# A decoder step on one core: sample scores, rank products and gate units reordered on TensorE, folded rows added on VectorE

## The reference

```python
z = h @ w_in                                   # q, k, v, conv inputs, gates
attn = sliding-window attention with sinks     # prompt blocks of 128; samples against cached keys
conv = c_b * short_conv(c_c * c_h)
h = layer_norm(ALPHA * h + (sigmoid(g_a) * (attn @ w_attn_out) + sigmoid(g_c) * (conv @ w_conv_out)) @ w_o)
eidx, gw = route(h, w_router, router_bias)     # 6 of 64 experts for each token
ffn = swiglu_shared(h) + sum over the 6 experts of gw * swiglu_e(h)
ple = sigmoid(h @ w_ple_gate) * (p @ w_ple_proj)
h = layer_norm(ALPHA * h + ffn + ple)          # the output y; keys, values and conv rows are outputs too
```

## Time and profile before

| | us |
|---|---|
| median of 3 runs | 1264.93 (1264.57 to 1266.1) |
| profiled execution, its time | 1267.28 |
| its span | 1265.4 |
| PE busy | 1227.0 (97%) |
| DVE busy | 497.9 (39%) |
| ACT busy | 306.3 (24%) |
| POOL busy | 159.8 (13%) |
| mean granted PE clock | 0.995 |

### The profile page before, as it was taken

How to read it: one execution, slowest core, us unless ns; L and a number is a source line. 1 busy time by engine, 2 the same in 40 slices (tenths; PEclk the granted TensorE clock), 3 DMA queues, 4 the chain that set the end, 5 groups by cost and what they waited for, 6 DMA issues and landing times.

```text
span 1265.4 us, 23325 instructions
## 1 busy us (share of the span) xinstructions
PE 1227.0 (97%) x8776; PEld 974.0 (77%) x8777; DVE 497.9 (39%) x1103; ACT 306.3 (24%) x560; POOL 159.8 (13%) x228
## 2 busy tenths in 40 slices
PE   7999999999999999999899999999999999999977
PEld 7988879999999999998899666556555566666643
DVE  4456574423453433566886112112112221111137
ACT  4344453322221222316012111111111111111121
POOL 0200000000000000004336121111111121211100
PEclk9999999999999999999999999999999999999999
DMA  9312122322223232606337999999999999999986
GB/s 279 103 37 67 34 68 51 80 71 79 89 68 100 67 109 76 211 21 208 141 115 305 420 419 419 421 421 419 420 421 419 420 421 418 420 421 421 421 351 264
DMA packets 98656, 307.31 MB, mean 243 GB/s; under 512 B 11244, under 2 KB 62404, under 8 KB 72840
## 3 DMA queue, kind: packets, MB, share of 16 engines
q1 hardware_dynamic: 85332, 275.20, 56.2%
q0 software_dynamic: 12304, 28.60, 5.8%
q10 hardware_dynamic: 948, 2.50, 0.6%
HBM read 294.45 MB, written 26.94 MB: 254 GB/s over the span
## 4 chain that ended last, share of the span: by engine, by line
PE 55%; DMA 37%; DVE 5%; issue 1%; DVEq 1%; ACT 0%; SPq 0%; POOL 0%; ACTq 0%; POOLq 0%
DMA w_exp<-in_w_e_down_dram 35%; PE proj L1051 32%; PE proj L1243 4%; PE proj L1384 3%; PE att L1454 2%; PE proj L1473 2%; PE att L1165 2%; PE att L1127 1%; DMA fold<-expert_rows 1%; PE att L1252 1%; PE proj L1338 1%; PE att L1178 1%; PE proj L1368 1%; PE proj L1077 1%; DVE res L2124 1%
## 5 line engine op out<-in xcount | busy, mean ns | idle before, releaser
L1454 PE MATMUL att<-w_exp,xt 128*64 128x256 f32 x2560 | 286.3, 380 | 2.7 <-DMA w_exp<-in_w_e_up_dram 2.1
L1454 PEld LDWEIGHTS att<-w_exp,xt 128*64 128x64 f32 x2560 | 207.6, 137 | 90.2 <-issue 27.5
L1051 PE MATMUL proj<-h_hi,w_hi 128*128 128x288 f32 x768 | 171.1, 304 | 0.0
L1051 PE MATMUL proj<-h_hi,w_lo 128*128 128x288 f32 x768 | 164.2, 295 | 0.0
L1051 PE MATMUL proj<-h_lo,w_hi 128*128 128x288 f32 x768 | 164.0, 295 | 0.0
L1473 PE MATMUL proj<-w_exp,ht_e 128*64 128x512 f32 x640 | 146.1, 597 | 9.6 <-DMA w_exp<-in_w_e_down_dram 4.9
L1051 PEld LDWEIGHTS proj<-h_hi,w_hi 128*128 128x128 f32 x768 | 122.0, 188 | 16.2 <-issue 15.2
L1051 PEld LDWEIGHTS proj<-h_lo,w_hi 128*128 128x128 f32 x768 | 123.5, 188 | 0.0
L1051 PEld LDWEIGHTS proj<-h_hi,w_lo 128*128 128x128 f32 x768 | 123.4, 188 | 0.0
L468 DVE TENSOR_TENSOR w_lo<-w_raw,w_hi 128x2048 fp32r<-128x2048 f32 x33 | 75.6, 2291 | 91.9 <-ACT w_hi L458 86.8
L1473 PEld LDWEIGHTS proj<-w_exp,ht_e 128*64 128x64 f32 x640 | 50.4, 136 | 77.7 <-issue 76.0
(11 more groups left out here) (384 smaller groups left out, 1810.8 us busy)
## 6 DMA issues: line engine op xcount, KB each, us to landing
w_exp<-in_w_e_gate_dram SPq DMA_DIRECT2D x64, 1024.0 KB, 16.9
w_exp<-in_w_e_up_dram SPq DMA_DIRECT2D x64, 1024.0 KB, 17.0
w_exp<-in_w_e_down_dram SPq DMA_DIRECT2D x64, 1024.0 KB, 17.1
w_raw<-in_w_in_dram SPq DMA_DIRECT2D x21, 1024.0 KB
part<-expert_rows SPq DMA_DIRECT2D x8, 1536.0 KB, 21.2
w_raw<-in_w_in_dram SPq DMA_DIRECT2D x8, 512.0 KB
w_raw<-in_w_attn_out_dram SPq DMA_DIRECT2D x8, 512.0 KB
w_raw<-in_w_conv_out_dram SPq DMA_DIRECT2D x4, 1024.0 KB
```

The source lines that it names most:

```text
L1051: last = nc.tensor.matmul(proj[:, 2 * i + a, 0:HALF], lhs, x[:, c, a * HALF:(a + 1) * HALF], start=(c == 0 and n == 0), stop=(c == KC - 1 ...
L1454: last = nc.tensor.matmul(att[e * SLOT:(e + 1) * SLOT, m, 0:FF], xt[:, c, e * SLOT:(e + 1) * SLOT], weights[e][:, c, :], start=(c == 0), s ...
```

## The change

Four edits. In the attention, PE's wait for the reading of the previous sample's scores moves from ahead of the sample scores to ahead of the prompt scores of the same step; ahead of the sample scores it waits for the one before that. In the routing, a third piece of the fourth quarter goes ahead of the rank products, and four gate units go ahead of the first table instead of three. In the end stage, DVE adds the three folded rows of tile 4 to one before it adds the sum of tile 0, and PE multiplies only that one; and a fourth row of tile 0 goes from DVE to PE.

```diff
-N_AHEAD = 3
+N_AHEAD = 4
...
-N_ON_PE = (3, 3, 4, 4)
+N_ON_PE = (4, 3, 4, 4)
...
                     if b == 0:
                         pe.wait_ge(qs_ready, 1)
-                    else:
-                        pe.wait_ge(sl_read, b)
+                    if b >= 2:
+                        pe.wait_ge(sl_read, b - 1)
                     pe.wait_ge(lg_read, n)
...
                     if n:
                         pe.wait_ge(lg_read, n)
+                    if n > 24:
+                        pe.wait_ge(sl_read, n - 24)
...
-            shared_half(1, 1, range(2))
+            shared_half(1, 1, range(3))
...
-            shared_half(1, 1, range(2, KC)).then_inc(su_ready, 1)
+            shared_half(1, 1, range(3, KC)).then_inc(su_ready, 1)
...
                 if t == NT - 1:
-                    pe.wait_ge(part_in[t], 16)
+                    pe.wait_ge(y_lo_ready, 2)
                     for half in range(2):
-                        for j in range(TOPK // 2):
-                            nc.tensor.matmul(out[:, half, :], fold_id[:, :], fold[:, j, half * 512:(half + 1) * 512],
-                                             start=(j == 0), stop=False)
+                        nc.tensor.matmul(out[:, half, :], fold_id[:, :], fold[:, 0, half * 512:(half + 1) * 512],
+                                         start=True, stop=False)
...
+            def fold_rows():
+
+                dve.wait_ge(part_in[NT - 1], 16)
+                nc.vector.tensor_tensor(fold[:, 0, :], fold[:, 0, :], fold[:, 1, :], ALU.add)
+                dve.drain()
+                nc.vector.tensor_tensor(fold[:, 0, :], fold[:, 0, :], fold[:, 2, :], ALU.add).then_inc(y_lo_ready, 1)
...
                 if s:
                     last_norm(s - 1, LAST_ORDER[s - 1])
+                if s == 0:
+                    fold_rows()
                 add_sum(s, t)
```

## The result

The changed kernel takes 1268.44 us (median of 20 runs, 1265.89 to 1270.38), the kernel before 1265.76 (20 runs, 1264.28 to 1267.25): a ratio of 1.0024, 95% interval 1.0018 to 1.0030. It is slower by a quarter of a per cent, where 1261.7 was forecast. Its runs also lie further apart, 4.5 us against 3.0. The profiled execution took 1269.49 us, span 1267.7.

What follows compares the result with a forecast made beforehand. PE bounds half of the end, transfers over a third; from 700 to 1204 the DMA engines are full. Gains of 0.77 + 0.8 (`routed`) + 1.2 + 0.5 = 3.3 us against 1264.93 gave 1261.7 us, range 1259.8 to 1264.0.

Steps and rivals of the forecast that it cites:

- the price at table 4: Routing: POOL's block 2 lies across DVE's table 4, so PE waits 1.4 us there (0 to 3.2).
- Rival (d): Routing: POOL holds table 4 for 5.2 us, PE idles 3.2, clock falls, `routed` 4.0 later: 1266.4 us; chance 0.05.
- the reorder: Routing: the moved piece and fourth unit bring PE's last table product, which releases `routed`, 2.18 us earlier before table 4's wait.
- rival (a): Routing: no collision on table 4, `routed` 2.18 us earlier: 1260.1 us; chance 0.18.
- The first table: Routing: PE's idle time ahead of the first table shrinks from 3.4 to 1.4 us; the clock stays up, gaining 2.98.
- rival (c): Routing: the clock falls in the new idle time at the first table too, 2.98 us given back: 1263.3 us; chance 0.07.
- The stream hole: Weight stream before 700: PE reaches the thin places earlier, so most of the hole closes, 1.2 us (0 to 1.4).
- Sample scores: Attention: the moved wait lets sample scores start earlier at even steps, 0.28 + 0.49 = 0.77 us (0 to 1.3).
- End stage: DVE's chain to tile 4's sum is later than PE's or even; gain 0.5 us (0.6 down to -0.4).
- rival (e): End stage: the clock stays up in most runs, so the end loses 1.1 us: 1263.3 us; chance 0.10.

Runs made afterwards that it cites:

- e1: The kernel before with the routing edits alone (third piece ahead of the ranks, four units ahead of the tables): 1.0014 of before.
- e3: The changed kernel with POOL's low part of block 2 made after unit 7 instead of unit 5: 1.0004 of before.
- e5: The changed kernel without POOL's low parts of blocks 2 and 3, ACT's copy in their place (low parts wrong): 0.9982 of before.
- e2: The changed kernel with the routing edits undone, so sample scores and end stage alone: 0.9997 of before.
- e7: The kernel before with the sample scores' edit alone: 0.9991 of before.
- e8: The kernel before with the two edits of the end stage alone: 0.9998 of before.
- e10: The kernel before with the third piece ahead of the rank products alone: 1.0003 of before.
- e6: The kernel before without POOL's low parts of blocks 2 and 3, ACT's copy in their place (low parts wrong): 0.9989 of before.
- e11: The changed kernel with POOL's low part of block 2 after unit 7 and that of block 3 behind `routed`: 1.0010 of before.
- e12: As e11, with the ranks ahead of the third piece again, as in the kernel before: 1.0003 of before.
- e16: The kernel before with the sample scores' edit and the routing edits, the end stage as before: 1.0007 of before.
- e4: As e3, with ACT's high part and POOL's low part of block 3 after unit 10 instead of unit 11: 1.0011 of before.
- e14: The changed kernel with a POOL memset of some 0.4 us ahead of block 2's low part: 1.0023 of before.
- e15: The changed kernel with a POOL memset of some 0.95 us ahead of block 2's low part: 1.0024 of before.
- e17: The kernel of e15 once more, unchanged, for a second profile: 1265.69 us in one run.
- e18: The changed kernel again, unchanged, for a third profile: 1268.2 us in one run.
- e9: The kernel before with the fourth gate unit ahead of the tables alone, the ranks as before: 1.0008 of before.

## Why the prediction was wrong, step by step

**The step that failed is the price at table 4.** The forecast was "PE waits 0.8 to 2.1 us; the bounds are 0 and POOL's whole 5.2 (3.2 of waiting). I take 1.4", with the clock untouched. The place and the mechanism were right: POOL's L708 lies across table 4, from 642.24, 28.4 us behind the ranks' copy (the forecast's 643.4 is 27.8 behind). The wait was 2.60, 2.60 and 1.99 in three profiles, inside the bounds and above the 1.4, and behind it the clock fell in two, which cost 3.06 and 1.79 more; the sum had nothing for that. POOL caught the weights ahead of the table as well, five DVE operations in all. Rival (d), which the prediction gave 0.05, is what happened in kind, though from less: it set the wait at 3.2 and its sign at an idle time of some 2.3 us, while the clock fell behind 1.99 in one execution and stayed up behind 2.60 in another. Its price, 1.5 us slower, was too low mainly for want of the second collision, below.

The trace of before could have told more: there the block had caught five operations, L1931 of the weights at 1.24 for 0.23 and the four of table 6, an excess of 3.9 us (650.57 to 656.66, less 2.23). The prediction read 2.85 from the table alone, allowed 1.3 more for the weights and took a value in the middle. With the slack of 2.0, which it had right, 3.9 is a wait of 1.9 us; the 4.5 of the changed kernel is the 2.60 measured. By the Trainium skill (SBUF — State Buffer, Who interferes with whom) a VectorE instruction with two SBUF inputs and a GpSimd one that reads SBUF shut each other out for their whole length, and a `tensor_scalar` can take the shared ports too; the trace agrees on both (1.45 for 0.44, L1932 1.35 for 0.23).

**A term was missing.** POOL's block 3 moved as well, onto DVE's last steps to `routed`: +1.5 us in the change, in e1 and in e3. I had dated block 2 against the tables and not block 3 against what lies behind them. e5 measures both collisions and the clock together: A 53.72 instead of 60.92, and 2.60 + 3.06 + 1.54 is the 7.20 between them. Against before e5's A is 2.43 shorter. The ranks come 0.8 later by the edit, so the reorder as such brings `routed` 1.6 us earlier where 2.18 was forecast, the place of rival (a).

**The first table** was right: idle 1.66 (forecast 1.4), and no low clock behind it in any profile with both routing edits, so rival (c) fell. The idle time is longer than forecast because POOL's work on the fourth unit lies on the table's last operation: L2001 took 0.99 for 0.44. The Trainium skill (TensorE: Matmul & The Clock Gate, A second HAM failure mode) would have PE throttled by frequent short idle times; the few idle times of 0.4 to 1.7 us that these routing stages have left it at 1.00.

**The stream hole** closed by about 0.8 (forecast 1.2, bounds 0 and 1.4), but not by the mechanism forecast. B is 541.7 to 542.1 in the five kernels that have three units ahead and POOL's block 3 behind `routed` (before, e2, e7, e8, e10), and 540.4 to 541.2 in those with four units and block 3 ahead of `routed`. e6 has three units and no block 3: 540.56. e11 and e12 have four units and block 3 behind `routed`: 543.3 and 543.7. So it is block 3 behind `routed` that thins the stream, and PE's head start, to which the prediction gave the 1.2, shows no part in it (e5 540.71 against e6 540.56). Block 3 cost 1.5 us ahead of `routed` in the change and gave back 0.8 behind it.

**Sample scores**: forecast 0.77, by the rows 0.7, by e7 1.1 (0 to 2.3). That the size came out is in part luck: the 0.28 of step 28, counted as lost, was kept, and step 30 gave some 0.2 instead of 0.49.

**End stage**: the profile gained 1.0 (forecast 0.5, DVE's chain the later: right). Against an old end stage that the clock spares it loses 0.7, which is rival (e), and e8 measures no difference.

**The sum.** Against the profile of before: 4.8 later at `routed` (A), 0.6 back (B), 1.0 back (C); the ranks came 0.9 earlier (1.0 is the start of the kernel; the 0.7 of the sample scores and the 0.8 of the piece all but cancel). The span is 2.3 longer. On this ruler the forecast for A was 1.6 shorter, so A missed by 6.4: 1.2 of wait, 3.06 of clock, 1.5 of block 3 and 0.6 of the reorder.

**Open.** The parts add to 1.0003 (e1, e7, e8), with some 0.0016 of uncertainty, and the whole is 1.0024 and 1.0023. Why the whole is more than its parts is not shown. The profiles do not part e1 and e16 from the change by their end stage. What differs is when block 2 lands: 5.5 and 5.7 us behind its issue, against 5.15, 5.16 and 5.23 in the change's three profiles. In the other seven profiles with the new end stage and the same program up to there (e3, e4, e5, e11, e14, e15, e17) it is 5.1 to 5.9, so this landing moves from execution to execution by more than the 0.35 us that parts a wait of 2.60 from one of 1.05. Counted from the ranks' copy, POOL's first operation came at 28.3 and 28.4 (waits 2.60), 28.4 (e18, 1.99), 28.7 (e14, 2.22), 28.7 (e1, 1.05), 28.9 (e16, 1.08), 29.4 and 29.6 (e15 and e17, 0.08 and 0). In e1 and e16 the table's first operation had begun when POOL did, by 0.08 and 0.33 us, and in the change's three profiles it had not. So e1 and the change may draw from much the same waits; whether that explains the whole difference of their medians is not shown.

The loss of e15's slow runs stays open as well: with the earliest landing seen its POOL would start at 29.1, where a long wait at table 4 is not to be expected. No version that does the whole work beat the kernel before by more than e7 (0.9991), which is the sample scores alone.

## What to carry to other kernels

Moving work on one engine moves the dates of all that it releases. List every operation of the other engines that hangs on the moved step, and for each date what it then lies across: here two blocks of POOL's, and the second one was forgotten. Look on both sides of the date: block 3 slowed the stream where it lay before, and `routed` where it lies now. Where an engine is held by another for whole instructions, count the instructions that come into reach, not the overlap. And price an idle time of PE with the clock's fall in it, as a chance: the wait of 1.05 us cost 1.3 in all, that of 2.60 cost 2.9 or 5.7.

## What the hardware showed that I had not expected

The same idle time does not always bring the same clock. After 2.60 us of idle the clock fell in one execution (3.06 us lost) and stayed in another (0.27); behind the 3.41 us at the first table of the kernel before, e2, e6, e7 and e8 it took between 1.7 and 3.0, and behind the 4.00 us of e10 1.77. Idle times of 1.66 us and less brought no fall in any profile of the routing stage. Kernels whose profile has an idle time of 1.99 us or more in the routing stage spread over 2.4 to 4.5 us; in e3, e5 and e11, where PE waits at most 0.64 for a table behind the first, the runs lie within 1.2 to 1.5 us. One profile doesn't tell the spread, though: e1, e4, e9, e12, e15 and e16, with table waits of 0.7 to 1.3 us and no fall in their profiles, spread over 2.1 to 4.9.

A 6-element-wide `tensor_scalar` on DVE, 0.23 us alone, took 1.35 beside a POOL subtraction: being short doesn't let an operation through.
